# One gate as the plain first projection, values as a quad, and softmax steps moved to the middle of blocks

## The reference, cut to what matters

```python
h = rmsnorm(x, norm_g)                        # x: 512 tokens x 2048
proj = h @ w_in                               # 4 x 1024 (branch A) + 9 x 1024 (B) + 1024 (bz) + 4 x 1024 (C) + 6144 (gates)
# A: 8 heads, two softmax maps each, causal, with ALiBi
p = softmax(s1) - lam * softmax(s2)
ya = rmsnorm(p @ av, subln_g) * (1 - lam_init) * silu(az)
# B: 8 heads, three groups (q, k, v each) of dilated windows, combined by their softmax denominators
yb = combined * silu(bz)
# C: short convolution
yc = cb * conv3(cc * cx) * silu(cz)
merged = g0 * (ya @ w_a) + g1 * (yb @ w_b) + g2 * (yc @ w_c)      # g = sigmoid(gates + gate_b)
out = rmsnorm(x + merged @ w_out, final_g)
```

## Time and profile before

| | before |
|---|---|
| median of 3 runs | 2505.21 us |
| profiled execution, its own time | 2505.15 us |
| its span (first to last instruction) | 2503.4 us |
| TensorE busy | 2484.4 us (99%) |
| VectorE busy | 1945.7 us (78%) |
| ScalarE busy | 1069.8 us (43%) |
| a looped head | 105.37 us |

### The profile page before, as it was taken

How to read it: one execution, slowest core, us unless ns; L and a number is a source line. 1 busy time by engine, 2 the same in 40 slices (tenths; PEclk the granted TensorE clock), 3 DMA queues, 4 the chain that set the end, 5 groups by cost and what they waited for, 6 DMA issues and landing times.

```text
span 2503.4 us, 30481 instructions
## 1 busy us (share of the span) xinstructions
PE 2484.4 (99%) x11454; PEld 2053.7 (82%) x11454; DVE 1945.7 (78%) x2266; ACT 1069.8 (43%) x1329; POOL 0.2 (0%) x4
## 2 busy tenths in 40 slices
PE   9999999999999999999999999999999999999998
PEld 8888888888888888888887788888878888788887
DVE  8797788566676767767678887788878888898875
ACT  5343333334333333333434433344444445655644
POOL 0000000000000000000000000000000000000000
PEclk9999999999999999999999999999999999999999
DMA  8255444686776667766535545445565456787666
GB/s 317 95 198 188 150 133 143 203 301 214 252 266 231 223 213 248 264 234 225 191 106 193 203 168 193 170 154 193 181 218 203 160 197 219 261 286 247 226 227 202
DMA packets 184902, 519.15 MB, mean 207 GB/s; under 512 B 14129, under 2 KB 59442, under 8 KB 181042
## 3 DMA queue, kind: packets, MB, share of 16 engines
q1 hardware_dynamic: 87872, 342.62, 39.9%
q10 hardware_dynamic: 96882, 174.55, 19.8%
HBM read 420.64 MB, written 96.47 MB: 207 GB/s over the span
## 4 chain that ended last, share of the span: by engine, by line
PE 92%; DVE 3%; DMA 3%; ACT 1%; issue 1%; DVEq 0%; ACTq 0%
PE proj L621 13%; PE proj L623 13%; PE proj L622 13%; PE sc_ps L621 6%; PE sc_ps L622 6%; PE sc_ps L623 6%; PE tr_ps L621 6%; PE tr_ps L622 6%; PE tr_ps L623 6%; PE o_ps L622 4%; PE o_ps L623 4%; PE o_ps L621 4%; PE tr_ps L664 1%; DVE w_lo L1547 1%; DMA rows<-c_dram 1%; DMA raw<-s_dram 1%
## 5 line engine op out<-in xcount | busy, mean ns | idle before, releaser
L1008 ACT ACTIVATE w_hi<-raw 128x1024 fp32r<-128x1024 f32 x296 | 314.0, 1061 | 430.3 <-PE proj L623 138.1
L1008 ACT ACTIVATE w_hi<-kb 128x1024 fp32r<-128x1024 f32 x280 | 297.2, 1062 | 442.6 <-PE proj L623 156.9
L1547 DVE TENSOR_TENSOR w_lo<-raw,w_hi 128x1024 fp32r<-128x1024 f32 x296 | 361.2, 1223 | 156.2 <-ACT w_hi L1008 155.3
L1547 DVE TENSOR_TENSOR w_lo<-kb,w_hi 128x1024 fp32r<-128x1024 f32 x280 | 342.7, 1224 | 116.6 <-ACT w_hi L1008 116.0
L621 PE MATMUL proj<-act_hi,w_hi 128*128 128x512 f32 x1024 | 405.8, 396 | 1.7 <-DVE w_lo L1591 1.7
L623 PE MATMUL proj<-act_hi,w_lo 128*128 128x512 f32 x1024 | 399.6, 390 | 0.0
L622 PE MATMUL proj<-act_lo,w_hi 128*128 128x512 f32 x1024 | 398.7, 389 | 0.0
L1057 ACT ACTIVATE w_hi<-raw 128x1024 fp32r<-128x1024 f32 x128 | 135.6, 1060 | 344.8 <-PE proj L623 339.9
L1591 DVE TENSOR_TENSOR w_lo<-raw,w_hi 128x1024 fp32r<-128x1024 f32 x128 | 156.6, 1224 | 103.1 <-ACT w_hi L1057 102.6
L623 PEld LDWEIGHTS proj<-act_hi,w_lo 128*128 128x128 f32 x1024 | 192.2, 188 | 41.3
L621 PEld LDWEIGHTS proj<-act_hi,w_hi 128*128 128x128 f32 x1024 | 192.8, 188 | 40.2 <-DVE w_lo L1591 1.9
(11 more groups left out here) (310 smaller groups left out, 4765.1 us busy)
## 6 DMA issues: line engine op xcount, KB each, us to landing
raw<-wg SPq DMA_DIRECT2D x128, 512.0 KB, 3.9
raw<-wst SPq DMA_DIRECT2D x128, 512.0 KB, 4.9
kb<-wg SPq DMA_DIRECT2D x28, 2048.0 KB, 7.6
ssum<-ws ACTq DMA_DIRECT2D x24, 2048.0 KB, 9.3
s_dram<-ssum ACTq DMA_DIRECT2D x24, 2048.0 KB, 7.7
raw<-s_dram SPq DMA_DIRECT2D x96, 512.0 KB, 4.4
raw<-ws SPq DMA_DIRECT2D x72, 512.0 KB, 4.1
kb<-wg SPq DMA_DIRECT2D x56, 512.0 KB, 6.3
```

Source lines behind the costliest of these rows:

```text
L1008: nc.scalar.activation(w_hi[r % RING][:, :], src, ACT.Copy).then_inc(hi_done, 1)
L1547: tt(w_lo[r % RING][:, :], src, w_hi[r % RING][:, :].bitcast(f32), ALU.subtract).then_inc(lo_done, 1)
```

## The change

Branch A's gate projection AZ, so far a block of each head, becomes the plain first projection. There the operands are exchanged (weights stationary, activations moving), so that its result has columns on partitions; it is stored unscaled to a new `z_dram`, loaded per head (`load_z`, 256 KB, in w = 6) and multiplied by `rstd` on DVE (`scale_z`). Branch A's values become a sixth quad ahead of the heads (`QUADS_V` 7 counts the plain one). A head has seven projected blocks (w = 2 to 8, BZ is 8) and 14 units, the loop round 42. The sums stand at n = 0, 4, 8 in head 0 and at 0, 4, ..., 36 in a round; the first of the 24 is made in the last quad before the heads, one add each in steps 13 to 16.

In the blocks w = 4 to 8 `scores_a`, `probs_a`, `probs_b` (c = 3) and `scores_b` (c = 0) move from behind the second unit to between the two units on TensorE, and `bias`, `exps`, `turned` on DVE and ACT ahead of the second split; `norm_a` follows in the same block. `inverse_a` and `norm_o` move from w = 4 to w = 3, `values_b` from w = 5 to w = 4, `values_a` stands behind w = 8. `scores_b` with c = 2 and 3 of the last head move into the quad behind the heads.

```diff
-NBLK1, NHU1 = 10, 16
+NBLK1, NHU1 = 9, 14
-QUADS_V, QUADS_C, QUADS_G, QUADS_O = 6, 10, 16, 2
-Q_AQ, Q_V = 1, 3
+QUADS_V, QUADS_C, QUADS_G, QUADS_O = 7, 11, 17, 2
+Q_AQ, Q_A, Q_V = 1, 3, 4
-SUMS_FIRST = (0, 4, 8, 12)
-SUMS_LOOP = (2, 6, 12, 16, 20, 24, 28, 34, 40, 44)
+SUMS_QUAD, SUM_QUAD_AT = 9, (13, 14, 15, 16)
+SUMS_FIRST = (0, 4, 8)
+SUMS_LOOP = (0, 4, 8, 12, 16, 20, 24, 28, 32, 36)
...
@@ plain_quad (TensorE)
-                            end = three(plain[half][b][:, :], act_hi[:, k, ts], act_lo[:, k, ts], w_hi[slot][:, cs], w_lo[slot][:, cs],
+                            end = three(plain[half][b][:, :], w_hi[slot][:, ws], w_lo[slot][:, ws], act_hi[:, k, :], act_lo[:, k, :],
...
@@ blocks (TensorE)
-                    if last and w == 9:
-                        values_a(i)
-                        probs_b(i, 0)
-                        scores_b(i, 1)
+                    if 4 <= w < 8:
+                        scores_a(i, w - 4)
+                    if w == BZ:
+                        scores_b(i, 0)
+                    if 5 <= w < 9:
+                        probs_a(i, w - 5)
+                    if w == 4 and not fresh:
+                        probs_b(i - 1, 3)
                     pe.wait_ge(lo_done, NHU1 * i + (R_H + t + 2))
                     multiply(h.bank(w), h.slot(t + 1), act_hi, act_lo, 8, False, True)
                     if w < 4 and not fresh:
                         scores_b(i - 1, w)
-                    if w < 5 and not fresh:
+                    if w < 4 and not fresh:
                         probs_b(i - 1, w - 1)
...
-                    if w == 5 and not fresh:
+                    if w == 4 and not fresh:
                         values_b(i - 1)
-                    if 4 <= w < 8:
-                        scores_a(i, w - 4)
-                    if 5 <= w < 9:
-                        probs_a(i, w - 5)
-                    if w == 8:
-                        scores_b(i, 0)
-                    if w == 9:
-                        if last:
-                            scores_b(i, 2)
-                        else:
-                            values_a(i)
-                            scores_b(i, 1)
-                            probs_b(i, 0)
+                    if w == BZ:
+                        values_a(i)
+                        scores_b(i, 1)
+                        probs_b(i, 0)
...
@@ quad behind the heads (TensorE)
-                            scores_b(HEADS - 1, 3)
+                        if n in (1, 3):
+                            scores_b(HEADS - 1, (n + 3) // 2)
...
@@ head (ACT)
+            def load_z(i):
+                act.dma_start(z_a[:, :], z_dram[bass.ds(i, 1), :, :].rearrange("o p q -> p (o q)")).then_inc(za_in, 16)
...
+                    if 5 <= w < 9:
+                        turned_a(i, w - 5)
+                    if w == 4 and not fresh:
+                        turned_b(i - 1, 3)
+                    if 4 <= w < 8:
+                        exps_a(i, w - 4)
+                    if w == BZ:
+                        exps_b(i, 0)
                     split(t + 1)
...
-                    if w == AZ:
+                    if w == 7:
                         tanh_half(i, AZ)
...
@@ head (DVE)
+            def scale_z(i):
+
+                dve.wait_ge(za_in, 16 * i + 16)
+                tt(z_a[:, :], z_a[:, :], rstd[:, :], ALU.mult).then_inc(z_scaled, 1)
...
                     if w < 5 and not fresh:
                         norm_b(i - 1, w - 1)
-                    if 5 <= w < 9:
-                        norm_a(i, w - 5)
-                    if w == 9:
-                        norm_b(i, 0)
                     split(t)
+                    if 4 <= w < 8:
+                        bias_a(i, w - 4, fresh)
+                    if w == BZ:
+                        bias_b(i, 0)
+                    if 5 <= w < 9:
+                        turned_a(i, w - 5)
+                    if w == 4 and not fresh:
+                        turned_b(i - 1, 3)
                     if w == Q0:
                         low_turn(h, AQ)
                     if w == K0:
                         low_turn(h, AK)
+                        if not fresh:
+                            inverse_a(i - 1)
+                            norm_o(i - 1)
...
                     if w == 4 and not fresh:
                         low_v(2 * i, v_b)
-                        inverse_a(i - 1)
-                        norm_o(i - 1)
...
-                    if w == 8:
+                    if w == BZ:
                         low_v(2 * i + 1, v_a)
-                    if w == 9:
                         silu(i, 0, AZ)
+                        norm_b(i, 0)
+                    if 4 <= w < 8:
+                        norm_a(i, w - 4)
                     scale_block(h, w)
+                    if w == 7:
+                        scale_z(i)
                     split(t + 1)
...
@@ quads ahead of the heads (DVE)
+                    if q == QUADS_V - 1 and n in SUM_QUAD_AT:
+                        sum_unit(0, SUM_QUAD_AT.index(n))
```

More of the change, by code:

```diff
@@ L52 @@
 TO_LINE, TO_LINE_1 = 24, 8
-AQ, AK, Q0, K0, Q1, K1, Q2, K2, AZ, BZ = range(NBLK1)
+AQ, AK, Q0, K0, Q1, K1, Q2, K2, BZ = range(NBLK1)
+AZ = NBLK1
 ENTRY = {AQ: 0, Q0: 1, AK: 2, K0: 3} | {b: b for b in range(Q1, NBLK1)}
@@ L1177, in head @@
                         comb_high(6, t2[0], f2, (comb_sum, 6))
-                    if last and w == 9:
-                        squares_o(i)
-                        turned_b(i, 0)
+                    if 5 <= w < 9:
[6 more added lines that the diff above has]
+                        exps_b(i, 0)
                     split(t + 1)
@@ L1195, in head @@
                             store_y(i - 1, 0, y_a)
+                        load_z(i)
                     if w == 7:
@@ L1201, in head @@
                             load_v(i, Q_V + g, v_g[g], vg_in, True)
-                    if w < 5 and not fresh:
+                    if w < 4 and not fresh:
                         turned_b(i - 1, w - 1)
-                    if 5 <= w < 9:
-                        turned_a(i, w - 5)
-                    if w == 9 and not last:
+                    if w == BZ:
                         turned_b(i, 0)
@@ L1310, in _ @@
                     end_of(q, n)
+                    if q == QUADS_V - 1 and n == SUMS_QUAD:
+                        act.wait_ge(pe_used, RING + first_unit(q) + 2 * NU)
+                        load_sums(0)
+                    if q == QUADS_V - 1 and n == SUM_QUAD_AT[-1] + 1:
+                        store_sums(0)
                     if q == QUADS_V - 1 and n == 16:
@@ L1578, in comb_low, with sum_unit @@
                 tt(dst, whole, hi.bitcast(f32), ALU.subtract).then_inc(comb_lo, 1)
-            def sum_units(m):
-                dve.wait_ge(osum_in, 16 * (m + 1))
-                link(tt(ssum[:, W22, :], ssum[:, W22, :], ssum[:, W21, :], ALU.add))
-                tt(ssum[:, W21, :], ssum[:, W21, :], ssum[:, W11, :], ALU.add)
-                link(tt(ssum[:, W11, :], ssum[:, W11, :], ssum[:, W22, :], ALU.add))
-                tt(ssum[:, W12, :], ssum[:, W12, :], ssum[:, W11, :], ALU.add).then_inc(osum_done, 1)
+            def sum_unit(m, step):
+                if step == 0:
+                    dve.wait_ge(osum_in, 16 * (m + 1))
+                    link(tt(ssum[:, W22, :], ssum[:, W22, :], ssum[:, W21, :], ALU.add))
+                if step == 1:
+                    tt(ssum[:, W21, :], ssum[:, W21, :], ssum[:, W11, :], ALU.add)
+                if step == 2:
+                    link(tt(ssum[:, W11, :], ssum[:, W11, :], ssum[:, W22, :], ALU.add))
+                if step == 3:
+                    tt(ssum[:, W12, :], ssum[:, W12, :], ssum[:, W11, :], ALU.add).then_inc(osum_done, 1)
+            def sum_units(m):
+                for step in range(4):
+                    sum_unit(m, step)
             def split_1(h, t):
@@ L1842, in head @@
                         join_b(i - 1)
-                    if w == 8:
+                    if w == BZ:
                         low_v(2 * i + 1, v_a)
-                    if w == 9:
                         silu(i, 0, AZ)
-                    if last and w == 9:
-                        turned_b(i, 0)
-                        bias_b(i, 1)
+                        norm_b(i, 0)
+                    if 4 <= w < 8:
+                        norm_a(i, w - 4)
                     scale_block(h, w)
+                    if w == 7:
+                        scale_z(i)
                     split(t + 1)
@@ L1853, in head @@
                         bias_b(i - 1, w)
-                    if 4 <= w < 8:
-                        bias_a(i, w - 4)
-                    if w == 8:
-                        bias_b(i, 0)
-                    if w < 5 and not fresh:
+                    if w < 4 and not fresh:
                         turned_b(i - 1, w - 1)
-                    if 5 <= w < 9:
-                        turned_a(i, w - 5)
                     if w == 3:
@@ L1864, in head @@
```

(14 more changed lines are left out.)

84 lines of the change are left out of this document (42 added, 42 removed).

## The result

The changed kernel takes 2560.02 us (median; 2558.62 to 2567.1), the kernel before in the same sessions 2504.3 us: ratio 1.0228, 95% interval 1.0208 to 1.0248. It is 55.7 us slower. The prediction said slower and 2535.0, with 2510 to 2550: the direction holds, the time lies 10 us above the range. The profiled run took 2558.62 us.

The account below looks back on a forecast made before the run. TensorE, busy 99%, bounds the kernel: number of matmuls by their spacing. 2505.15 − 10.9 + 20.0 + 4.0 + 6.0 + 3.4 + 3.0 + 0.5 + 2.1 + 0.7 + 1.0 = 2535.0 us; range 2510 to 2550.

Parts of the forecast that it names:

- The arithmetic: On TensorE's path: 16 head units removed, one quad added, net 48 matmuls fewer, −10.9 us; 0.7 us of DVE backlog shows.
- First place: Blocks K0 and Q1: TensorE waits 1.8 and 3.2 us around scores of A, four heads, 20.0 us; second heads 4.0 us.
- the sum of 2.0: Second head of each round: 0.6 us for delayed normalisation plus 1.4 us before `values_b`; two heads, 4.0 us.
- Second place: Last block, BZ: `values_a` waits, 6.0 us for the second heads and 3.4 us for first and third heads.
- The term of the second heads' BZ: A sum unit in BZ makes `values_a` 2.8 us late, with its load 3.0 us, twice: 6.0 us.
- a late `values_a`: BZ of first and third heads: ACT's split late or held, 1.2 and 0.5 us, each twice, 3.4 us; bounds 0 and 12.
- The rest: Head 7 3.0 us, head 0 0.5, scores left over after the heads 2.1, more breaks in the matmul stream 1.0.
- the tail quad: After the heads two scores are left over; the second's bias stands behind two splits: 2.1 us (0 to 4).
- The clock falls: Rival: half speed follows each of four pause places, 2.5 us lost each time, 2535 + 10 = 2545 us; chance 0.09.
- a sign of being wrong: Granted clock under 1.00 inside the heads would show the rival in which the clock falls, chance 0.09.
- the likeliest case: Whole kernel: waits as worked out, at full clock, 2535.0 us; own range 2520 to 2548; chance 0.69.
- The other side: Rival: DVE's lead absorbs the waits in the heads, only some 3 us left, 2497 us; chance 0.13.

Follow-up runs that it names:

- Runs 2 and 3: Changed kernel with inverse_a and norm_o of heads 1, 3, 4, 6 back in block Q1: 2537.7 us; changed kernel without the heads' sum-unit adds: 2509.0 us.
- run 5: Changed kernel with the next head's branch A mask load issued at the end of BZ instead of block 7: 2559.2 us, ratio 1.0226.
- run 1: Changed kernel with extra matmuls, results unread, keeping TensorE at work in its long pauses: 2541.8 us, ratio 1.0156.
- Run 6: Changed kernel with TensorE's loop over the two rounds of heads written out, other engines keeping theirs: 2555.1 us, ratio 1.0204.
- run 7: Changed kernel with sum units at units 5, 9, 13 of looped heads, four in head 0, two in the last quad, mask load at BZ's end: 2522.0 us.
- run 8: Changed kernel with run 7's sum-unit places and later mask load, and TensorE's loop written out too: 2520.1 us, ratio 1.0072.

## Why the prediction was 25 us short

Step by step, measured in the trace of the changed kernel.

- *The arithmetic*, −10.9 us, holds: 48 matmuls fewer, the new quad at 76.2 us, nothing added by its four adds (0.7 forecast, worked out with 5.3 us for split and copy, for which it shows no row), heads of 94.9 us once the waits are away.
- *First place.* Forecast 1.8 and 3.2 us in heads 1, 3, 4 and 6, measured 1.7 and 3.2 in each: 20 us, as forecast. Runs 2 and 3 show the cause: VectorE's order there, with a sum unit in K0. In the second heads `values_b` waits 1.9 us, where 1.4 had been worked out, and the 0.6 us ahead of it, for `pr`, don't appear: the sum of 2.0 is right in part by luck.
- *Second place.* The term of the second heads' BZ was too small: 3.0 us each forecast, 5.4 and 3.8 measured. Of the difference in head 2, 1.8 us are the issue of the mask load (runs 5 and 1), a transfer that stood in the code beside the moved steps and that I hadn't costed, though the earlier trace rows have an idle time of 4.57 us ended by issuing. For the first and third heads I forecast a late `values_a`, 3.4 us in all; it isn't late there. There are five small waits of the scores of B for K2 instead, 2.1 us.
- *The rest.* Head 7 waits 2.5 us (3.0 forecast), the tail quad 2.2 and 1.1 (2.1), the turn of AK 0.6 us twice (none). *The turn of the round* wasn't in the sum: 5.2 us for 1.7 before. Run 6 shows that it is TensorE's jump; why the jump of the kernel before hides in 1.7 us stays open, no run tried it.
- *The clock falls*: this is the step that failed. The sum had TensorE at full clock behind every wait; I gave the fall 0.09 as a rival, with four falls of 2.5 us, 10 us. It happened nine times and costs 17.5 us by the account; run 1, which takes away eight of the falls and leaves the jump's, gives back 18.2 us, of which 13.5 are the clock. What the prediction named as a sign of being wrong, a granted clock under 1.00 inside the heads, is what the trace shows. The reason against it, that the scores of A break each pause in two, had no row behind it: the few short matmuls between 1.7 and 3.2 us of idleness didn't keep the clock. Nor was the pause of 3.2 us the point from which it happens: the same 1.9 us before `values_b` were followed by 0.50 in head 5 and not in head 2; what decides there stays open. The rule of the Trainium skill that I weighed (TensorE: Matmul & The Clock Gate, HAM oscillation) has the falls right at nine of the ten places in the heads where TensorE stood for 1.9 us or more (head 2's `values_b` is the tenth, and the 2.2 us in the quad behind the heads had no fall either), and I should have let it decide the likeliest case, since no row of the kernel before showed a pause of over 1.7 us that the clock outlived. The rival itself, as it stood, gave 2545 us: its price for a fall was too high (2.5 for 1.9 us in the mean) and its count too low. Nine falls at 2.5 us would have made 2535 + 22.5 = 2557.5 us, but the nine can be counted only afterwards: one of them lies at the jump, which wasn't in the sum at all.
- The other side, waits absorbed by VectorE's lead, did not come to pass where a sum unit stood beside the moved steps in K0, Q1 or BZ; the units in the other blocks were hidden.

So of the 25 us, some 17 are the clock, 3.5 the turn of the round, 3.2 the second heads' BZ, and the rest small terms of both signs.

## What to carry to other kernels

Where a forecast puts pauses into the stream of matmuls, price the clock with them: a few short matmuls between two pauses don't keep it, and each fall took 1.5 to 2.6 us on top of the wait. When steps are moved ahead in one engine's program, lay every other engine's queue of that stretch beside them, its large adds and its DMA issues: the work was hidden by where it stood. The six looped heads took 627 us in the changed kernel and 579 us with 18 of their 20 sum units at other places and one transfer issued later (run 7, which pays for the other two in head 0 and the last quad; the times from the turn of AQ of head 1 to that of head 7). And before trading matmuls for other placement, ask for the best case: without any of the adds this change gains nothing, because the pauses at the turn of the round, in head 7 and behind the heads take what the 48 matmuls give.

## What the runs showed of the hardware

- Issuing a transfer can take long by itself. The mask load, 0.35 to 0.37 us at its later place in run 5, took 5.4 and 3.7 us in heads 2 and 5 of the changed kernel, right behind a 2 MB load and three smaller transfers on the same queue, and ScalarE stood idle for 5.0 and 3.3 of them. In the other heads, where no 2 MB load is issued in that block, it took 1.25 to 1.4 us. No run changed the 2 MB load alone.
- TensorE's jump back to the start of a long loop body took 4.2 to 5.3 us in seven of the kernels here, at most 1.7 us in the kernel before, and nothing with the body written out; it counts as a pause for the clock too, whose granted value fell to 0.50 at 958.8 us in the changed kernel.
- Extra matmuls into a free bank, in time that would be waited anyway, kept the clock at 1.00 there; of the 18 us that came back some 13.5 are the clock.
- Shorter pauses can be followed by 0.50 too. Two of 1.2 and 1.4 us were, in head 0 of run 7 (at 604 us), and two of 1.6 and 1.4 us at the same place in run 8 were not.
